# Twelve row products of each expert layer moved from VectorE to GpSimd and ScalarE

## The reference, cut to what matters

```python
def peer_ffn(xn, wq, sub_keys, u_tab, v_tab):
    q = jnp.matmul(xt, wq)...reshape(t, PEER_HEADS, 2, PEER_SUBDIM)
    scores = jnp.einsum('thcd,hcnd->thcn', q, sub_keys)
    ...                                   # top 16 twice: idx and best_s, 8 heads x 16 experts a token
    gate = jax.nn.softmax(best_s, axis=-1)
    act = jnp.einsum('td,thkd->thk', xb, u_tab[ib])
    wgt = jax.nn.gelu(act) * gb
    return jnp.einsum('thk,thkd->td', wgt, v_tab[ib])
```

## Time and profile before

| | us |
|---|---|
| median of 3 runs | 2328.86 |
| lowest and highest run | 2324.53, 2336.24 |
| the profiled execution | 2322.81 |
| its span, first to last instruction | 2320.8 |
| TensorE busy | 2185.4 |
| VectorE busy | 1210.0 |
| GpSimd busy | 464.1 |
| ScalarE busy | 431.1 |

### The profile page before, as it was taken

One profiled execution on the slowest core, in us unless ns is written; L12 is line 12 of the kernel. 1 busy time (PEld: TensorE's weight loads), 2 busy tenths in 40 slices (PEclk: granted clock), 3 DMA queues, 4 the chain that ended last, 5 costly groups with the idle time before them and its releaser, 6 DMA issues. The chain is left out here.

```text
span 2320.8 us, 32591 instructions
## 1 busy us (share of the span) xinstructions
PE 2185.4 (94%) x13344; PEld 1951.6 (84%) x13344; DVE 1210.0 (52%) x2470; ACT 431.1 (19%) x1035; POOL 464.1 (20%) x410
## 2 busy tenths in 40 slices
PE   7998699998988999999999997998999999999998
PEld 4465488886667899999999997667899999999998
DVE  3255421112642796888644443542596877744443
ACT  3013310001241103443100000242112442200000
POOL 0000000000000013444533330000012444433331
PEclk9999899999988999999999998988999999999999
DMA  9135123443422488999999995322288999999996
GB/s 369 51 148 206 73 91 132 158 163 113 164 86 91 150 312 343 390 398 399 403 409 409 407 407 226 145 110 91 109 304 319 395 380 373 412 409 409 406 408 255
DMA packets 113525, 616.38 MB, mean 266 GB/s; under 512 B 10201, under 2 KB 10585, under 8 KB 95322
## 3 DMA queue, kind: packets, MB, share of 16 engines
q1 hardware_dynamic: 55578, 403.31, 44.3%
q0 software_dynamic: 57504, 208.82, 23.6%
q10 hardware_dynamic: 288, 2.10, 0.3%
HBM read 612.16 MB, written 2.03 MB: 265 GB/s over the span
## 5 line engine op out<-in xcount | busy, mean ns | idle before, releaser
L390 PE MATMUL psum<-HT,arena 128*128 128x160 f32 (+1 forms) x5984 | 994.0, 327 | 15.4 <-DVE HT L1644 7.1
L390 PEld LDWEIGHTS psum<-HT,arena 128*128 128x128 f32 x5984 | 924.7, 191 | 69.2 <-issue 18.3
L390 PE MATMUL psum<-arena 128*128 128x160 f32 (+6 forms) x5850 | 879.6, 312 | 37.2 <-DMA arena<-in_peer_v 13.9
L390 PEld LDWEIGHTS psum<-arena 128*128 128x128 f32 (+2 forms) x5850 | 814.2, 193 | 86.9 <-issue 32.3
L1962 DVE SCALAR_TENSOR_TENSOR arena<-arena,small 128x1024 f32<-128x1024 f32 x180 | 231.3, 1285 | 288.0 <-DMA arena<-in_peer_v,small 275.9
L2062 POOL DMA_INDIRECT arena<-in_peer_u,small x192 | 246.6, 1284 | 318.2 <-DVE small L1913 281.4
L2062 POOL DMA_INDIRECT arena<-in_peer_v,small x192 | 203.6, 1060 | 363.3 <-PE psum L390 206.9
L1913 DVE CUSTOM_DVE_ANT_0 arena<-arena 128x1024 f32<-128x1024 f32 x192 | 228.7, 1222 | 57.1 <-DMA arena<-in_peer_u,small 52.7
L2068 POOL DMA_DIRECT2D row_tokens<-arena x2 | 1.2, 623 | 1090.9 <-ACT arena L957 1090.9
L390 PE MATMUL psum<-arena,HT 128*128 128x384 f32 (+3 forms) x544 | 199.3, 526 | 7.0 <-DVE HT L1644 7.0
L957 ACT ACTIVATE arena<-psum 128x512 f32<-128x512 f32 (+6 forms) x130 | 64.9, 513 | 653.4 <-PE psum L425 333.3
(11 more groups left out here) (227 smaller groups left out, 996.6 us busy)
## 6 DMA issues: line engine op xcount, KB each, us to landing
arena<-in_peer_ut SPq DMA_DIRECT2D x64, 2048.0 KB
arena<-in_peer_v SPq DMA_DIRECT2D x64, 2048.0 KB
arena<-in_w_mod SPq DMA_DIRECT2D x12, 2048.0 KB
arena<-in_w_in SPq DMA_DIRECT2D x16, 1536.0 KB
arena<-in_w_up SPq DMA_DIRECT2D x11, 2048.0 KB
arena<-in_peer_wq SPq DMA_DIRECT2D x8, 2048.0 KB
arena<-in_w_out SPq DMA_DIRECT2D x6, 2048.0 KB
arena<-in_w_down SPq DMA_DIRECT2D x11, 1024.0 KB
```

What stands on the lines that cost most here:

```text
L390: return pe.matmul(o, a, b, start=start, stop=stop, skip_group_check=True)
```

## The change

For the first twelve rows of a layer (`POOL_ROWS`) the dot of VectorE is taken apart. GpSimd multiplies the gathered buffer by the tokens in place (`row_product`). ScalarE copies the buffer onto itself with an accumulator that sums it into `ACTV` (`row_sum`), one row after each of the slots 9 to 20 (`SUM_LAG` = 9). The first gathers into buffers that these rows used wait for `row_summed` instead of `rows_used`, and stand between the products on GpSimd's queue. The counts of `rows_used` are lowered by twelve. VectorE's dots begin at row 12, and `DOTS_BEFORE` goes from 9 to 21, so nine dots still stand before the first one-hots and two after each gated slot.

```diff
+POOL_ROWS, SUM_LAG = 12, 9
-DOTS_BEFORE, DOTS_NUM = 9, 4
+DOTS_BEFORE, DOTS_NUM = 21, 4
...
                 def row_activations(g):
-                    act.wait_ge(rows_used, (g + 1) * TOPK)
+                    act.wait_ge(s("row_summed"), POOL_ROWS)
+                    act.wait_ge(rows_used, (g + 1) * TOPK - POOL_ROWS)
...
+                def row_sum(n):
+                    act.wait_ge(s("row_product"), n + 1)
+                    act.activation(GR[n % RING], GR[n % RING], ACT.Copy, accum_out=ACTV[:, n:n + 1]
+                                   ).then_inc(s("row_summed"), 1)
+
                 for m in range(PAIRS_U):
                     expert_activations(m)
+                    if 0 <= m - SUM_LAG < POOL_ROWS:
+                        row_sum(m - SUM_LAG)
                     if m == EXP_AFTER:
...
-                row_dots(0, 2)
+                row_dots(POOL_ROWS, 2)
                 dve.wait_ge(s("best_exp"), 1)
...
-                row_dots(2, DOTS_BEFORE - 2)
+                row_dots(POOL_ROWS + 2, DOTS_BEFORE - POOL_ROWS - 2)
...
-                        if m >= RING:
-                            pool.wait_ge(rows_used, m - RING + 1)
+                        if RING <= m < RING + POOL_ROWS:
+                            pool.wait_ge(s("row_summed"), m - RING + 1)
+                        elif m >= RING:
+                            pool.wait_ge(rows_used, m - RING - POOL_ROWS + 1)
...
-                gathers("peer_u_2", 0, RING + 2)
+                def row_product(n):
+                    j = n % RING
+                    pool.wait_ge(gathered[j], layer * slot_uses(j) + (n // RING + 1) * 16)
+                    pool.sem_inc(tick, 1)
+                    pool.tensor_tensor(GR[j], GR[j], XNG[:, 0, :], ALU.mult).then_inc(s("row_product"), 1)
+
+                gathers("peer_u_2", 0, RING)
+                pool.wait_ge(s("rows_moved"), layer * (16 + RGROUPS * 16) + 48)
+                pool.sem_inc(tick, 1)
+                for n in range(POOL_ROWS):
+                    row_product(n)
+                    if n >= 2:
+                        gathers("peer_u_2", RING + n - 2, 1)
+                at = RING + POOL_ROWS
+                gathers("peer_u_2", at - 2, 2)
                 pool.wait_ge(s("gate_ready"), 1)
                 move_out(1, GATE, "gate_moved")
-                gathers("peer_u_2", RING + 2, 6)
+                gathers("peer_u_2", at, 6)
                 move_in(1, GG, "gate_moved")
-                gathers("peer_u_2", RING + 8, ROWS - RING - 8)
+                gathers("peer_u_2", at + 6, ROWS - at - 6)
```

More of the change, by code:

```diff
@@ L308, in build @@
             "ml_w", "ml_p", "expm", "sg_squared", "sg_v", "o_exp", "ws_masked", "y2_squared", "y2_mean",
-            "y2_rooted", "y2_ready", "best_sub", "best_exp", "idx_ready", "rows_moved", "onehot_raw", "idx_moved", "gate_ready", "gate_moved",
+            "y2_rooted", "y2_ready", "best_sub", "best_exp", "idx_ready", "row_product", "row_summed", "rows_moved", "onehot_raw", "idx_moved", "gate_ready", "gate_moved",
             "onehot", "g_stored", "w_first", "acts_in", "v_used", "row_acts", "yp_ready",
@@ L1909, in row_dots @@
                         g, j = n // TOPK, n % RING
-                        if n % TOPK == 0:
+                        if n % TOPK == 0 or n == POOL_ROWS:
                             dve.wait_ge(s("rows_moved"), layer * (16 + RGROUPS * 16) + 16 + max(g + 1, 2) * 16)
@@ L1962, in row_sums @@
                             dve.scalar_tensor_tensor(y, GR[j], w, y, ALU.mult, ALU.add).then_inc(rows_used, 1)
-                        dve.wait_ge(rows_used, m + 1)
+                        dve.wait_ge(rows_used, m + 1 - POOL_ROWS)
                         if n % TOPK == TOPK - 1:
@@ L2024, in _, with slot_uses @@
                 [v for k, v in S2.items() if k not in ("idx_moved", "gate_moved", "rows_moved")] + [rows_used]
+            def slot_uses(j):
+                return len(range(j, 2 * ROWS, RING)) * 16
             with pool.Fori(0, LAYERS) as layer:
```

## The result

| | before | after |
|---|---|---|
| median of 20 runs | 2331.12 us (2324.53 to 2340.46) | 2344.20 us (2334.53 to 2350.09) |
| profiled execution | 2322.81 us, span 2320.8 | 2343.98 us, span 2342.2 |
| mean granted clock in it | 0.969 | 0.963 |

The ratio of after to before is 1.0056, with a 95% interval of 1.0044 to 1.0068: the change makes the kernel 0.6% slower. The forecast of 2328 us, no change that can be seen, was wrong: the medians differ by 13.1 us where 0.7 us less was forecast. The measured time lies inside the range of 2315 to 2352 us, on its slower side.

What follows compares the result with a forecast made beforehand. TensorE, busy 94% of the span, was taken as the bound, with DMA behind its expert-stage waits. +13.2 us at first gate tiles and -13.9 us of value-tile waits gave -0.7 us, so 2328 us, range 2315 to 2352.

Steps and rivals of the forecast that it cites:

- Part 1: Products of rows 0 to 11 on GpSimd: 2.6 us each, fitting up to 3.5 us, cost on the path 0.
- rival A: GpSimd products take over 3.5 us and set the pace of the sums; at 4.5 us, 2351 us; chance 0.13.
- Rival B: Products delay VectorE's choosing 15 us; selections lose up to 5.5 us a layer, deciding beyond 9.5 us; 2339 us; chance 0.08.
- Part 2: Row sums on ScalarE: 1.5 us each, twelve fitting in its idle time, cost 0.
- Part 3: Gathers moved into the DMA's gap: one every 4.35 us, 361 GB/s below the 409 it holds, no tile late, cost 0.
- Part 4: New wait at the first gate tile, because dot 20 needs gather 20: 6.6 us a layer, +13.2 us.
- L: Time from issue of gather 20 to its row at hand before the first gate tile, taken as 6.8 us.
- rival C: Gather 20's row takes 12 us or more to arrive: 2338 us at 12, 2362 at 23.8; chance 0.10.
- Part 5: Late stalls: TensorE's waits for value tiles early in the value stages vanish, -13.9 us; 7.4 us of one-hot waits stay.
- D: Rival: value-stage stalls stay, since the same bytes pass and demand just equals the DMA's rate; 2342 us; chance 0.12.
- The clock ... is no term: In TensorE's stretches the clock is 1.00 outside the stalls, so no clock cost was counted.

Runs made afterwards that it cites:

- nine_products: After with nine GpSimd products instead of twelve, DOTS_BEFORE 15, gathers only behind runs of one or two products: 2311.57 against before's 2326.25 us, 0.9931.
- no_products: After without the twelve multiplications on GpSimd, row sums adding the bare rows, every wait kept: 2327.79 against before's 2330.49 us, 0.9986.
- dots_17: After with DOTS_BEFORE 17 instead of 21, so five dots instead of nine before the first one-hots: 2326.30 against before's 2330.49 us, 0.9979.
- before_with_products: Before with eight products added in GpSimd's idle time, gathers, sums and dots left in place: 2350.31 against before's 2330.49 us, 1.0083.
- early_dots_12: Before with twelve VectorE dots moved between calls of choose, DOTS_BEFORE 19, exponential and selections after slots 18 and 20: 2323.46 us, 0.9977 of before.

## Why the prediction was wrong

The step that failed is the last sentence but one of **Part 1**, "Cost on the path: 0". It priced a product by whether GpSimd could fit it in. That was right: 2.37 us each against 2.6 taken and a limit of 3.5, so rival A is out. What it left out is what the product does to VectorE: the choosing ends 14.8 us later, and TensorE waits 5.2 us in each layer at the selections, where 0 was taken. **Rival B** named it and had 0.08: choosing 15 us late and 5.5 us a layer at the selections were its numbers. That they came so near is luck. B counted nineteen two-input products between 1729 and 1762, from calls of choose of 9.6 us; the calls lie 13.8 us apart in before (L1886 at 1744.75, and then at 1758.51), which makes fourteen, and 11 us at B's own 0.8 us each. Its point of decision, 9.5 us, held in five kernels whose order of selections is that of before (late, and the wait at the selections, layer 2): 7.6 us and 0; 7.7 and 0; 14.8 and 5.2; 16.4 and 6.8; 18.0 and 7.1. Layer 1 of nine_products, 11.4 us late, waits 1.8. The chance was too low: the one row that bore on it, the gathers stretched from 0.95 to 1.96 us beside VectorE's dots, spoke for B, and none spoke against it. The mechanism was imagined too mildly as well. B let each two-input product of VectorE lose 0.8 us; in the runs shifts and casts are held too, and a shift for several products together.

The Trainium skill, "SBUF — State Buffer", Who interferes with whom, says that GpSimd and VectorE's two-input and faster copy-like forms exclude each other, and that reductions never contend. The rows of L1888, L1896 and L1906 agree with it. By this rule the wait at the selections was to be forecast, and should have been a term of the sum.

**Part 2** held: a sum is 1.05 and 0.19 us against 1.5, and costs nothing itself. But ScalarE did wait, which this part did not foresee: 11.60 us before the exponential, with the sums 8 to 11 behind it. By no_products it cost nothing at the first gate tile.

**Part 3**: the gap was filled, 415 GB/s from 1740 to 1760 of after and 412 from 1756 to 1776, which is the stretch for which 360 was forecast, 16 us later. The DMA is full there (share 1.00), where the forecast left it slack.

**Part 4**, right in its mechanism and too small by L. Gather 20 went out at 1807.76 and its row was used at 1817.87: 10.1 us (10.6 in layer 1), where 6.8 was taken; rival C's 12 is nearer. Why L is 10 us was not tried; the late sums are not the reason, as in no_products, where the gathers ahead go out one a slot, it is 11.2 (from 1799.59 to 1810.82). This term is +18.0 us at the first gate tiles instead of +13.2. dots_17 shows that it belongs to the nine dots: with five of them before the one-hots the one-hot waits fall by 16.1 us although the choosing is as late. no_products shows that it needs no late choosing: 9.0 and 9.9 us without.

**Part 5** was right and rather too small: no value wait in after, and 12.5 us of them in before_with_products, where no row is moved ahead. The two value stages are 19.6 us shorter, 13.9 of waits and 5.7 of TensorE's busy time at a granted clock of 1.00. What those 5.7 us were in before is not shown. D is out.

**"The clock ... is no term"** was wrong by some 6.9 us, TensorE's additional busy time from the selections to the end of the score stages; its rows right behind the new waits are at 1.2 GHz. A new wait of 5 us or more was priced at its length alone.

So the sum for the expert networks should have read: 19.6 us of gain against 18.0 at the first gate tiles, 10.4 at the selections, 6.9 of clock and 0.8 at later one-hots. That is +16.5, where the profiled executions show +15.6 and the medians +13.1.

## What to carry to other kernels

An idle GpSimd is no free engine beside a busy VectorE: eleven products there delayed VectorE's own work by 14.8 us, 1.3 us each, no less than VectorE's own twelve dots in the same place (early_dots_12: 14.1 us, 1.2 each). In a run of eight without a gather between them it was 18.0 us, 2.3 each. The gain of this change is in the gathers moved into the DMA's gap (the two value stages are 19.6 us shorter in after, and 1.7 in before_with_products, which moves none), and this can be had without the new work: six more dots on VectorE itself give 0.9939 of before's time, nine products on GpSimd with the dots cut to 15 give 0.9931, the same within their intervals.

When rows are moved ahead, move the work that asks for them too only as far as they can be there: DOTS_BEFORE of 17 instead of 21 was worth 18 us by itself. And a wait on the bounding engine is priced with the slow matmuls behind it.

## What the runs showed of the hardware

A shift of VectorE that meets GpSimd's product waited for the end of GpSimd's whole run of back-to-back products, not of one: 18.15 us for 0.18 us of work beside eight, 5.36 beside three. A gather issued between two products lets it in, as at 1751.66. Beside single products casts of 128x64 (0.72 to 1.26 us in after instead of 0.20), two-input products and dots (3.37 instead of 1.22) are held too. No cast of 128x32 met a product. The searches (MAX8, FIND_INDEX8, MATCH_REPLACE8) are not held: the longest of them takes 0.43 us in before and in after alike. The other way round, products on GpSimd were stretched little: 2.35 to 2.49 us over all 24 of them; the two longest are the twelfth of each layer, which start while a dot is running.
